# Wide attention tiles: the combination of two maps moved ahead of the next maxima, the first copy ahead of both exponentials, and drains of projected rows moved behind divisions

## The reference

```
A: y_a = rg_lru(causal_conv(a_x)) * silu(a_g)              # 512 channels, a scan over the tokens
B: keys are scored by a light indexer; the 256 best per query are kept;
   y_b = softmax(q k^T over the kept keys) v * silu(b_g)   # 4 heads of 64
C: s = q k^T per half head, chunk mask; p = softmax(s)     # 4 heads, two maps p[0], p[1] each
   attn = p[0] - lam * p[1]
   y_c = rmsnorm(attn v, subln) * (1 - lam_init) * silu(c_g)
mix = concat(y_a, y_b, y_c) @ w_out ;  x = x + rmsnorm(mix, norm_post)
```

## Time and profile before

| | us |
|---|---|
| median of 3 runs (lowest, highest) | 1707.88 (1705.3, 1713.13) |
| the profiled execution, its own time | 1700.6 |
| its span, first to last instruction | 1698.8 |
| PE busy | 1579.7 (93%) |
| DVE busy | 1135.0 (67%) |
| ACT busy | 629.6 (37%) |
| POOL busy | 429.1 (25%) |

### The profile page before, as it was taken

How to read it: one execution, slowest core, us unless ns; L and a number is a source line. 1 busy time by engine, 2 the same in 40 slices (tenths; PEclk the granted TensorE clock), 3 DMA queues, 4 the chain that set the end, 5 groups by cost and what they waited for, 6 DMA issues and landing times. The chain is left out here.

```text
span 1698.8 us, 21027 instructions
## 1 busy us (share of the span) xinstructions
PE 1579.7 (93%) x7298; PEld 1085.2 (64%) x7298; DVE 1135.0 (67%) x2456; ACT 629.6 (37%) x1227; POOL 429.1 (25%) x540
## 2 busy tenths in 40 slices
PE   6999999999979798989989999999998888999887
PEld 4566566678867665666556666666887767466663
DVE  3478999967955645555345899999487455455551
ACT  3276621218043323433316753212452333233340
POOL 2000620530012244431410043233100212445311
PEclk9999999999989999999999999999999798999999
DMA  5100000321050212111411000113101303111101
GB/s 176 54 22 20 34 25 27 115 70 51 0 184 7 112 32 63 44 38 32 158 56 54 25 25 25 50 56 100 56 26 58 130 9 112 45 50 56 50 12 52
DMA packets 38888, 98.13 MB, mean 58 GB/s; under 512 B 8640, under 2 KB 27584, under 8 KB 34432
## 3 DMA queue, kind: packets, MB, share of 16 engines
q1 hardware_dynamic: 38784, 96.80, 17.2%
HBM read 65.79 MB, written 18.14 MB: 49 GB/s over the span
## 5 line engine op out<-in xcount | busy, mean ns | idle before, releaser
L1697 PE MATMUL ps<-r_xn,r_w 128*128 128x384 f32 (+1 forms) x1728 | 555.6, 473 | 11.8 <-DVE r_xn L1353 6.3
L1697 PEld LDWEIGHTS ps<-r_xn,r_w 128*128 128x128 f32 x1728 | 326.4, 191 | 195.3 <-issue 14.6
L1454 DVE TENSOR_SCALAR_CACHE_REDUCE r_ix<-r_sc,smi 128x768 bf16<-128x768 f32 (+6 forms) x380 | 342.0, 962 | 2.2
L1255 ACT ACTIVATE r_sc<-ps,sm 128x1024 f32<-128x1024 f32 (+8 forms) x204 | 156.1, 765 | 305.8 <-DVE sm L1588 305.4
L1588 DVE TENSOR_REDUCE sm<-ps 128x1 f32<-128x1024 f32 (+8 forms) x204 | 159.7, 786 | 120.3 <-PE ps L1856 55.6
L1773 PE MATMUL ps<-r_w,r_xn 128*128 128x256 f32 x1024 | 223.4, 380 | 0.0
L1773 PEld LDWEIGHTS ps<-r_w,r_xn 128*128 128x128 f32 x1024 | 194.1, 190 | 27.1 <-issue 1.0
L1893 PEld LDWEIGHTS ps<-r_vg,r_w 128*128 128x128 f32 (+1 forms) x1176 | 156.1, 201 | 56.7 <-issue 25.8
L1874 PE MATMUL ps<-ident,r_sc 128*128 128x128 f32 (+1 forms) x684 | 120.4, 287 | 62.6 <-DVE r_sc L641 47.5
L1874 PEld LDWEIGHTS ps<-ident,r_sc 128*128 128x128 f32 (+1 forms) x684 | 85.2, 150 | 133.8 <-issue 102.4
L1893 PE MATMUL ps<-r_vg,r_w 128*128 128x64 f32 (+1 forms) x1176 | 157.4, 280 | 7.5 <-DVE r_w L657 4.9
(11 more groups left out here) (254 smaller groups left out, 2057.3 us busy)
## 6 DMA issues: line engine op xcount, KB each, us to landing
r_w<-w_in SPq DMA_DIRECT2D x28, 1024.0 KB, 5.0
r_xn<-w_out SPq DMA_DIRECT2D x2, 4096.0 KB, 13.4
y<-r_res SPq DMA_DIRECT2D x16, 512.0 KB, 2.9
r_vg<-x SPq DMA_DIRECT2D x8, 512.0 KB, 10.0
r_xn<-ckT SPq DMA_DIRECT2D x2, 2048.0 KB, 8.5
r_xn<-vcache SPq DMA_DIRECT2D x2, 2048.0 KB, 14.2
o_v<-r_vg SPq DMA_DIRECT2D x4, 1024.0 KB, 10.9
r_sc<-x SPq DMA_DIRECT2D x8, 512.0 KB, 4.8
```

The costliest lines, as they stand in the source:

```text
L1255: ins = nc.scalar.activation(ex[2 * (i % 2) + m][0:r, 0:w], on_slot(("qk", i, m), w, r), ACT.Exp, bias=negm[0:r, c:c + 1], accum_out=den[0 ...
L1454: ins = vec.tensor_scalar(unsel[t][0:rows(t), :], sc[t][0:rows(t), :], b, None, op, ALU.add, accum_out=cnt[0:rows(t), c:c + 1])
L1697: ins = nc.tensor.matmul(on_ring(key, cn), w[:, k, P * s:P * (s + 1)], xnT[:, k, c0:c0 + cn], start=(k == 0), stop=(k == KT - 1))
```

## The change

Three lines of `schedule()` are edited, and a branch is split in two. In wide C heads the combination goes ahead of the next head's maps, and the copy of the first transposes goes ahead of both exponentials of the next head. In wide B heads the first transposes go ahead of a second map of the next unit. In all wide heads the drain goes behind the first transposes, and in narrow tiles behind the division.

```diff
@@ -185,7 +185,7 @@
         if len(groups) == 1:
             head = one[:-1] + ytr + one[-1:] + own if plain else own + one[:-1] + ytr + one[-1:]
-            steps += head + take(i, 1) + pv + rows_now + two + take(i, quota - 1) + groups + div
+            steps += head + take(i, 1) + pv + two + take(i, quota - 1) + groups + div + rows_now
@@ -197,9 +197,12 @@
+        elif plain:
+            steps += one[:-1] + ytr + one[-1:] + own + take(i, 1) + groups[:1] + two + rows_now
+            steps += take(i, quota - 1) + pv + div + groups[1:]
         else:
-            steps += one[:-1] + ytr + one[-1:] + own + rows_now + two[:-1]
-            steps += take(i, 1) + groups[:1] + two[-1:] + take(i, quota - 1) + pv + div + groups[1:]
+            steps += own + one[:-1] + ytr + two[:-1] + take(i, 1) + groups[:1] + rows_now + one[-1:] + two[-1:]
+            steps += take(i, quota - 1) + pv + div + groups[1:]
```

## The result

| | before | changed |
|---|---|---|
| median of the runs, us | 1710.5 (4 runs, 1705.3 to 1718.5) | 1639.5 (4 runs, 1637.6 to 1644.4) |
| profiled execution, us (span) | 1700.6 (1698.8) | 1644.4 (1642.6) |
| mean granted clock of the profiled execution | 0.975 | 0.992 |
| PE busy, us; PE idle (span less busy), us | 1579.7; 119.1 | 1554.5; 88.1 |
| time at the lower clock level, us | 83 | 26 |

The ratio is 0.9585, 95% interval 0.954 to 0.9631: 4% faster. Measured again later in five rounds, beside three other kernels, the changed kernel gave 0.9599 (0.9561 to 0.9637), 1640.8 us. One of the six executions of that series, at 2027.7 us and a clock of 0.747, was in a slower state and is left out. The last row of the table is summed over windows of 1 us: in each, the time at the lower level is (1 - clock) / 0.5.

What follows compares the result with a forecast made beforehand. TensorE, busy 93%, bounds the kernel, so gains come from its idle time or clock. 32.3 + 16 - 1.3 = 47 us off 1700.6 gives 1653.6; with 7.3 added 1660.9, rounded to 1660, range 1644 to 1688.

Steps and rivals of the forecast that it cites:

- the clock term: Wide C-head stretches: lower clock level costs 21 us, of which 16 us come back, bounds 0 and 21.
- the 7.3 us added to get from the trace to the median: Whole kernel: the median before, 1707.88, was 7.3 us above the profiled 1700.6, so 1653.6 became 1660.9.
- The loop: 32 wide C heads: combination first shortens PE's waits, a tile 7 head takes 5.7 us; gain 32.3 us.
- The drains: DVE's drains of projected tiles moved behind copies or divisions: -0.65 us per layer, -1.3 us in all, a loss.
- (e): Unit 29: the drain waits for POOL in either order, so nothing, between +0.9 and -0.9 us.
- (a): Unit 36: the product's wait of 0.93 us for a division queued behind the drain goes, +0.9 us.
- (b): Unit 67: the last transposes' wait of 1.31 us for the copy goes, +1.2 us.
- (c): Unit 50: the next tile's first projection step waits for the later drain, -2.15 us.
- (d): Unit 58: the division's second step still runs under POOL's later addition; copy and PE's next transposes 0.6 us later.
- rivals 1 and 4: Clock does not come back, 1677 us, chance 0.20; clock sinks in the wide stretches, 1776 us, chance 0.04.
- rival 2: C heads' new loop is 0.7 us longer per head; half the idle and clock loss stay, 1686 us, chance 0.14.
- rival 3: No change within 0.5%: loop and drains eat the gain, a tile 7 loop of 7.0 us; 1705 us, chance 0.04.

Runs made afterwards that it cites:

- the narrow drains: Changed kernel with the drains of the narrow tiles alone put back ahead of the next head's second map: 1650.7 us, ratio 0.9654 to the kernel before.

## Why the prediction was right or wrong

The forecast was 1660 us in a range from 1644 to 1688; measured were 1639.5, and 1640.8 the second time. It was too high by 20, just beyond the range's end. The side and the mechanism were right. Two steps of the sum failed in size: the clock term, which left out stretches at the lower level, and the 7.3 us added to get from the trace to the median. Of the 21 us by which the unrounded 1660.9 missed, 9 are the first and 12 the second.

- **The loop** (combination, transposes, copy, two exponentials; 5.7 us in tile 7): 5.55 in the trace. The waits left were to be 0, 0.5, 0.8, 0.8, 1.5, and are 0, 0.45 (for the slot), 0.80, 0.71, 1.35; in tile 6 the forecast 1.2, 1.0, 1.0, 0.3 stands beside 1.25, 0.53, 0.77, 0; tile 4 keeps 0.2 of 3.5. The 32.3 us of this term are 34.8 (35.7 less twice 0.45 for the slot).
- **A wait not thought of:** a faster tile 7 and 6 reaches the first projection step before `w_out` has landed, 1.09 and 2.71 us. Of this load the prediction said only that SP's order stays. It took 3.8 of the 34.8 back. That the idle time of the two traces differs by 31.0, the very sum predicted (32.3 - 1.3), is luck: the loop gave 2.5 more and the drains 4.8 more (below), `w_out` took 3.8, and by difference 3.5 are spread over other waits.
- **The drains** (-1.3) came out at about +3.5 in the traces: L1893's waits fell by 5.2 and those for L614's copy by 1.9, and the drain's new ones are 3.6. The step that failed is (e), unit 29. "The drain waits for POOL in either order: nothing" overlooked that the copy and the division no longer wait with it, and that POOL's addition then misses the next combination. That was bounded by a neighbour's row and not read at its own place, where the kernel before shows the wait of 1.53: 2.9 us a layer, and with the clock beside it most of the 10 us of the narrow drains. Steps (a) and (b) were right, 0.93 and 1.31 gone. So was (c), 1.80 for the 2.15 forecast. In (d) the sum was near by two errors: the wait of 1.40 for the copy behind the drain fell to 0.20, a gain of the kind of (b) that was not counted, and the division's step grew from 1.69 to 2.27 and made the next transposes wait 1.59, which was priced at 0.6. The net loss is 0.4.
- **The clock** (16 of 21 us) is 25 us between the traces and an estimated 31 between the medians. The 21 us counted only the lower level in wide stretches, 48 of the 83 us at it. Of those 48, 41 went, which at 0.39 to 0.46 is 16 to 19 us: the 16 taken was about right. What failed is what it left out. The windows of the kernel before that hold the waits of units 29 and 30 are at the lower level too, for 17 us in all, and read 1.00 in the changed kernel: 7 to 8 us more.

```profile
642.00:650.00 8.00, 7.03 (x20) 3.87 (x20) 5.56 (x15) 2.41 (x9) 4.08 (x4) 0.57 0.49 131
1476.00:1490.00 14.00, 10.97 (x32) 6.13 (x32) 8.27 (x22) 4.03 (x16) 6.65 (x9) 0.63 0.28 77
```

- **From the trace to the median:** 7.3 us were added because the profiled execution lay so far under the median, as if the changed kernel would keep that distance. It did not: its own profiled execution lies 5 us above its median. Clock is part of it: 0.975 in the profiled execution and 0.973 in the median one are 3.2 us by the line. The rest stays open. At its clock the profiled execution of the kernel before lies 5 us under the line, whose scatter is 1.9, and that of the changed kernel 4 above another execution with the same 0.992.
- **The rivals:** the clock came back (rivals 1 and 4 did not happen), the loop was not longer (rival 2), and the time moved by far more than 0.5% (rival 3). The filled gaps show that the clock's part was no accident.

The Trainium skill's "TensorE: Matmul & The Clock Gate", section "A second HAM failure mode: psum-queue depth-cycling", was weighed as a rule by which gaps of 0.8 to 1.0 us would keep the clock swinging. In tiles 7 and 6 of layer 0, gaps of 0.5 to 1.35 us left it at 1.00. Shortening the gaps of the kernel before brought its clock up, so the rule's cause stands and its reach at this length of gap does not show here.

## What to carry to other kernels

Where the clock dips in a profile, price each idle gap twice: by its own length and by the clock it costs, here 25 us of clock beside 31 of idle time between the traces. Take all stretches at the lower level, not only those of the loop being changed. If the profiled execution lies off the median, don't carry the distance over to the changed kernel as a fixed offset: here it was 7 us one way before and 5 the other way after. Take what a higher clock explains of it, and widen the range by the rest. And when an instruction that waits for another engine is moved on its queue, ask of each instruction that stood behind it whether it still waits, and beside what it now runs.

## What the runs showed of the hardware

- More work made the kernel faster: 320 matmuls of 128x128 in PE's waits took 23 us off 1708, by the clock alone (0.973 to 0.987 as a mean of the executions; both kernels lie on one line of time against clock).
- A DVE instruction of two SBUF inputs that starts under POOL's addition ends with it or up to 0.3 us behind it. L674 (before: L671) on 128x64 takes 0.23 us alone, and 1.69 and 2.27 under POOL's 2.35 and 2.34; L644 on 128x256 takes 0.48 alone and 2.45 under it. The Trainium skill, "SBUF — State Buffer", section "Who interferes with whom", says that such an instruction contends with a GpSimd one that reads SBUF; this trace agrees.
- With waits of mostly 1.5 to 3.2 us in the heads of tiles 7 and 6 the clock fell in some stretches and not in others (tile 6 at 1.00 and 0.78). With waits up to 1.35 us it held in three of four. In the fourth it fell right behind the wait of 2.71 us for `w_out`, at 1380 us, and so it did in the second trace of the changed kernel, at 1381 behind a wait of 2.89. What decides between two stretches alike stays open.
